# Ten adaLN panels in the inner norm gaps, and decays, samples and turned outputs as 128-row products, in a hybrid decoder step on one core

## What is computed

```python
def _layer(x, c, st, p):
    mod = silu(c) @ p['ada_w'] + p['ada_b']            # 1024 -> 9 * 1024
    sh1, sc1, g1, sh2, sc2, g2, sh3, sc3, g3 = split(mod, 9)
    u = modulate(rmsnorm(x, p['norm_ff1']), sh1, sc1)
    x = x + 0.5 * g1 * ((silu(u @ w1) * (u @ w3)) @ w2)
    u = modulate(rmsnorm(x, p['norm_mix']), sh2, sc2)
    mq, mk, mv, mo, mi, mf, z, xbc, dtp, ga, gb = split(u @ p['w_in'])
    # branch a: causal conv and silu of q and k, mLSTM with matrix memory C (samples start from a state),
    #           head norm, sigmoid(mo), @ w_pa -> ya
    # branch b: causal conv and silu of xbc, state-space scan with decays
    #           lmat = exp(cum[t] - cum[s]), y = (C B^T * lmat) @ (dt x) + exp(cum) * C @ h0, gate, norm, @ w_pb -> yb
    merged = sigmoid(ga) * ya + sigmoid(gb) * yb
    x = x + g2 * (merged @ p['w_out'])
    u = modulate(rmsnorm(x, p['norm_ff2']), sh3, sc3)
    x = x + 0.5 * g3 * ((silu(u @ w1b) * (u @ w3b)) @ w2b)
    return x, states
```

## Time and profile before

| | us |
|---|---|
| median of 3 runs | 1436.12 (1432.69 to 1439.61) |
| the profiled execution | 1435.53 |
| its span, first to last instruction | 1433.8 |

### The profile page before, as it was taken

The page is one execution under the profiler, slowest core; times in us unless marked ns, Lnnn a source line. Parts: engine busy times, 40 slices in busy tenths (PEclk is TensorE's granted clock), DMA queues, the critical chain, the costliest instruction groups (busy, mean ns, idle before and its releaser), DMA issues. The chain is left out here.

```text
span 1433.8 us, 22800 instructions
## 1 busy us (share of the span) xinstructions
PE 1329.5 (93%) x9262; PEld 1199.7 (84%) x9262; DVE 771.7 (54%) x1344; ACT 610.6 (43%) x1070; POOL 146.4 (10%) x282
## 2 busy tenths in 40 slices
PE   5699999997989987888999999999999879999997
PEld 2599999995988855557998878888999879999997
DVE  0544444436975555554368666855365464555542
ACT  3433334224546443434345554544463244333333
POOL 3000000000320011110013121111100010000000
PEclk9799999998999998999999999999999999999999
DMA  9566666764433377893463354463334353544441
GB/s 277 196 206 220 221 218 204 232 228 147 147 95 89 128 269 260 274 319 102 147 206 118 111 162 140 133 196 114 114 102 133 132 176 119 177 147 138 142 144 56
DMA packets 258606, 241.54 MB, mean 168 GB/s; under 512 B 8399, under 2 KB 242215, under 8 KB 258454
## 3 DMA queue, kind: packets, MB, share of 16 engines
q1 hardware_dynamic: 249198, 211.00, 47.2%
q0 software_dynamic: 8832, 28.91, 5.7%
q10 hardware_dynamic: 472, 0.17, 0.0%
HBM read 209.84 MB, written 30.21 MB: 167 GB/s over the span
## 5 line engine op out<-in xcount | busy, mean ns | idle before, releaser
L1817 DVE TENSOR_TENSOR w_lo<-ring,w_hi 128x1024 fp32r<-128x1024 f32 (+1 forms) x264 | 336.1, 1274 | 510.5 <-ACT w_hi L1302 509.4
L1302 ACT ACTIVATE w_hi<-ring 128x1024 fp32r<-128x1024 f32 (+1 forms) x264 | 289.4, 1097 | 604.0 <-PE bank L659 597.2
L659 PE MATMUL bank<-u_hi,w_hi 128*128 128x320 f32 x1536 | 278.6, 325 | 24.7 <-ACT u_hi L1334 19.6
L659 PEld LDWEIGHTS bank<-u_hi,w_hi 128*128 128x128 f32 x1536 | 239.8, 194 | 43.4 <-issue 27.6
L659 PE MATMUL bank<-u_lo,w_hi 128*128 128x320 f32 x1536 | 263.2, 315 | 0.0
L659 PE MATMUL bank<-u_hi,w_lo 128*128 128x320 f32 x1536 | 258.4, 311 | 0.0
L659 PEld LDWEIGHTS bank<-u_lo,w_hi 128*128 128x128 f32 x1536 | 240.2, 193 | 0.0
L659 PEld LDWEIGHTS bank<-u_hi,w_lo 128*128 128x128 f32 x1536 | 235.6, 189 | 0.0
L563 POOL TENSOR_TENSOR arena<-arena 128x320 f32<-128x320 f32 x24 | 20.9, 871 | 653.3 <-ACT arena L1314 640.5
L659 PE MATMUL bank<-arena 32*128 32x128 f32 (+6 forms) x600 | 63.8, 376 | 22.3 <-DMA arena<-in_state_mlstm_C 18.5
L656 PE MATMUL aux<-ident,arena 128*128 128x128 f32 (+5 forms) x389 | 58.6, 274 | 11.3 <-ACT arena L1353 8.9
(11 more groups left out here) (327 smaller groups left out, 1514.9 us busy)
## 6 DMA issues: line engine op xcount, KB each, us to landing
ring<-in_w_in SPq DMA_DIRECT2D x52, 1024.0 KB, 5.2
ring<-in_ff_w SPq DMA_DIRECT2D x44, 1024.0 KB, 5.2
ring<-in_ada_w SPq DMA_DIRECT2D x36, 1024.0 KB, 7.3
ring<-in_ff_w SPq DMA_DIRECT2D x32, 704.0 KB, 4.5
arena<-in_state_mlstm_C SPq DMA_DIRECT2D x32, 512.0 KB, 4.5
out_s_C<-arena POOLq DMA_DIRECT2D x32, 512.0 KB, 4.8
ring<-in_w_pa SPq DMA_DIRECT2D x8, 1024.0 KB, 5.4
arena<-in_state_ssm SPq DMA_DIRECT2D x32, 256.0 KB, 3.7
```

Source lines behind the costliest of these rows:

```text
L659: return nc.tensor.matmul(dst, lhs, rhs, start=first, stop=last)
L1302: nc.scalar.activation(w_hi[v.split_no % 2][:, 0:v.kc, :], panel_part(v), ACT.Copy).then_inc(S["hi_done"], 1)
L1817: V.tensor_tensor(w_lo[r][:, 0:v.kc, :], panel_part(v), w_hi[r][:, 0:v.kc, :].bitcast(FP32), ALU.subtract)\
```

## The change

- Gap 2 has six adaLN panels (26 to 31) instead of three, gap 3 four (32 to 35) instead of two; up1 has 12 instead of 14, down1 six instead of seven, up2 none instead of two.
- `high_ahead` and `low_ahead` take a last unit that they don't go beyond. In down1 and out it is that stage's own last unit. In the gaps ACT makes the next stage's first w_hi between the pairs of tiles, the second one at the end, and DVE the w_lo likewise.
- `norm_high` works by pairs of tiles, `normed` is cut into the reciprocal, a half and a range of u_lo tiles; rows and sums of the panels stand between these parts. The first norm calls the same parts one after the other.
- The decay product takes all 128 rows: rows 0 to 63 of head_pick and cum_rows are filled with zeros by DVE. cum_rows shared its columns with xd_s, which therefore moves over tri and tri_s, no longer used by then.
- The sample products take 128 instead of 96 rows of vp, kpm and st_s, with the last 32 rows filled with zeros by ACT. `turn_head` transposes all 128 rows of the third block.

Of the diff, hunks without their context; the order of the parts inside norm_high and normed is as told above:

```diff
@@ -31,10 +31,9 @@
-ADA_HEAD, ADA_GAP2, ADA_GAP3 = range(0, 8), range(29, 32), range(32, 34)
-ADA_AFTER_UP = dict(zip((3, 5, 9, 11, 15, 17, 21, 23, 27, 29, 33, 35, 39, 41), range(8, 22)))
-ADA_AFTER_DOWN = {2 * a + 1: 22 + a for a in range(7)}
-ADA_AFTER_UP2 = {3: 34, 9: 35}
+ADA_HEAD, ADA_GAP2, ADA_GAP3 = range(0, 8), range(26, 32), range(32, 36)
+ADA_AFTER_UP = dict(zip((3, 7, 11, 15, 17, 21, 23, 27, 31, 35, 39, 41), range(8, 20)))
+ADA_AFTER_DOWN = {2 * a + 1: 20 + a for a in range(6)}
@@ -123,10 +122,7 @@
-    for q in range(2 * KF):
-        order.append(("up2", q))
-        if q in ADA_AFTER_UP2:
-            order.append(("ada", ADA_AFTER_UP2[q]))
+    order += [("up2", q) for q in range(2 * KF)]
@@ -165,6 +161,8 @@
+        with nc.sbuf_tensor("xd_s", [128, 512], FP32) as xd_s:
+            pass
@@ -312,7 +310,6 @@
-        xd_s = part(14592, 512)
@@ -965,7 +962,7 @@
-                    mm(q[32 * g:32 * g + 32, :], st_s[h][0:96, 384 + 32 * g:416 + 32 * g], vp[g][h][0:96, :].bitcast(FP32), True, False)
+                    mm(q[32 * g:32 * g + 32, :], st_s[h][:, 384 + 32 * g:416 + 32 * g], vp[g][h][:, :].bitcast(FP32), True, False)
@@ -985,7 +982,7 @@
-                        ins = mm(pair[:, d, :], kpm[(SB * h + k) % 4][0:96, d * 128:(d + 1) * 128], vp[g][h][0:96, :])
+                        ins = mm(pair[:, d, :], kpm[(SB * h + k) % 4][:, d * 128:(d + 1) * 128], vp[g][h][:, :])
@@ -1013,7 +1010,7 @@
-                turn(x[:, 256:320], nm[0:64, 2, j * 128:(j + 1) * 128], 64).then_inc(S["hn_turned"], 1)
+                turn(x[:, 256:384], nm[:, 2, j * 128:(j + 1) * 128], 128).then_inc(S["hn_turned"], 1)
@@ -1089,7 +1086,7 @@
-                    mm(x[:, 0:448], head_pick[64:128, n:n + 1].to_broadcast([64, 128]), cum_rows[64:128, :], True, False)
+                    mm(x[:, 0:448], head_pick[:, n:n + 1].to_broadcast([128, 128]), cum_rows[:, :], True, False)
@@ -1246,15 +1243,8 @@
-            before = None
-            for u in st.range(("up2", 0), ("up2", 2 * KF - 1)):
-                if u.name == "ada":
-                    ada(u)
-                else:
-                    dense(u, norm=2 if u.q == 0 else None)
-                if before and before.name == "ada":
-                    mod_columns(before)
-                before = u
+            for u in st.of("up2"):
+                dense(u, norm=2 if u.q == 0 else None)
@@ -1291,11 +1281,13 @@
-            def high_ahead(u):
+            def high_ahead(u, last=units[-1]):
+                    if v.n > last.n:
+                        break
@@ -1321,17 +1313,17 @@
-            def norm_high(n, shift):
+            def norm_high(n, shift, pair):
+                tiles = range(2 * pair, 2 * pair + 2)
...
@@ -1401,16 +1394,25 @@
-                high_ahead(u)
+                high_ahead(u, st.at["down1", 2 * KD - 1])
-            for u in st.range(("ada", ADA_GAP2[0]), ("ada", ADA_GAP2[-1])):
-                ada_row(u)
-                if u.q == ADA_GAP2[0]:
-                    root(1)
-            norm_high(1, 3)
+            fill = [st.at["ada", a] for a in ADA_GAP2]
+            ada_row(fill[0])
+            root(1)
+            ada_row(fill[1])
+            ada_row(fill[2])
+            norm_high(1, 3, 0)
+            ada_row(fill[3])
+            norm_high(1, 3, 1)
+            ada_row(fill[4])
+            high_ahead(fill[-1], st.at["qk", 0])
+            norm_high(1, 3, 2)
+            ada_row(fill[5])
+            norm_high(1, 3, 3)
+            high_ahead(fill[-1])
@@ -1498,10 +1500,13 @@
-                copy(st_s[h][64:96, 416:448], st_s[h][32:64, 416:448]).then_inc(S["sx_ready"], 1)
+                ch.inc(copy(st_s[h][64:96, 416:448], st_s[h][32:64, 416:448]))
+                copy(st_s[h][96:128, 384:448], st_s[h][96:128, 0:64], scale=0.0).then_inc(S["sx_ready"], 1)
+                for g in range(2):
+                    ch.inc(copy(vp[g][h][96:128, :], seg_b[96:128, :, :].rearrange("p b t -> p (b t)"), scale=0.0))
@@ -1542,6 +1547,7 @@
+                    ch.inc(copy(kpm[n][96:128, :], seg_b[96:128, 0:4, :].rearrange("p b t -> p (b t)"), scale=0.0))
@@ -1752,19 +1758,23 @@
+                high_ahead(u, st.at["out", KD - 1])
+                square(2, u.own)
+            fill = [st.at["ada", a] for a in ADA_GAP3]
+            ada_row(fill[0])
+            root(2)
+            ada_row(fill[1])
+            norm_high(2, 6, 0)
+            ada_row(fill[2])
+            norm_high(2, 6, 1)
+            ada_row(fill[3])
+            high_ahead(fill[-1], st.at["up2", 0])
+            norm_high(2, 6, 2)
+            norm_high(2, 6, 3)
+            high_ahead(fill[-1])
+            for u in st.of("up2"):
-                square(2, u.own)
-            for u in st.range(("ada", ADA_GAP3[0]), ("ada", ADA_GAP3[-1])):
-                ada_row(u)
-                if u.q == ADA_GAP3[0]:
-                    root(2)
-            norm_high(2, 6)
-            for u in st.range(("up2", 0), ("up2", 2 * KF - 1)):
-                high_ahead(u)
-                if u.name == "ada":
-                    ada_row(u)
-                else:
-                    up(u, KF)
+                up(u, KF)
@@ -1807,11 +1817,13 @@
-            def low_ahead(u):
+            def low_ahead(u, last=units[-1]):
+                    if v.n > last.n:
+                        break
@@ -1830,18 +1842,21 @@
-            def normed(n, shift):
+            def inverse_root(n):
...
+            def normed(n, shift, half):
...
+            def normed_low(n, first, end):
...
@@ -1908,15 +1926,27 @@
-                low_ahead(u)
+                low_ahead(u, st.at["down1", 2 * KD - 1])
-            normed(1, 3)
-            for a in ADA_GAP2:
-                mod_add(st.at["ada", a])
+            fill = [st.at["ada", a] for a in ADA_GAP2]
+            inverse_root(1)
+            mod_add(fill[0])
+            normed(1, 3, 0)
+            mod_add(fill[1])
+            normed(1, 3, 1)
+            mod_add(fill[2])
+            normed_low(1, 0, 2)
+            mod_add(fill[3])
+            normed_low(1, 2, 4)
+            low_ahead(fill[-1], st.at["qk", 0])
+            mod_add(fill[4])
+            normed_low(1, 4, KD)
+            low_ahead(fill[-1])
+            mod_add(fill[5])
@@ -2204,6 +2234,7 @@
+                ch.inc(V.tensor_scalar(head_pick[0:64, :], ones[0:64, 0:32], 0.0, None, ALU.mult))
@@ -2226,6 +2257,7 @@
+                ch.inc(V.tensor_scalar(cum_rows[0:64, :], seg_b[0:64, 0:7, :].rearrange("p b t -> p (b t)"), 0.0, None, ALU.mult))
@@ -2401,19 +2433,24 @@
+                low_ahead(u, st.at["out", KD - 1])
+                residual(u, KD)
+            fill = [st.at["ada", a] for a in ADA_GAP3]
+            inverse_root(2)
+            mod_add(fill[0])
+            normed(2, 6, 0)
+            mod_add(fill[1])
+            normed(2, 6, 1)
+            mod_add(fill[2])
+            normed_low(2, 0, 2)
+            mod_add(fill[3])
+            normed_low(2, 2, 4)
+            low_ahead(fill[-1], st.at["up2", 0])
+            normed_low(2, 4, KD)
+            low_ahead(fill[-1])
+            for u in st.of("up2"):
-                residual(u, KD)
-            normed(2, 6)
-            for a in ADA_GAP3:
-                mod_add(st.at["ada", a])
-            before = None
-            for u in st.range(("up2", 0), ("up2", 2 * KF - 1)):
-                low_ahead(u)
-                if u.name != "ada":
-                    up(u)
-                if before and before.name == "ada":
-                    mod_add(before)
-                before = u
+                up(u)
```

More of the change, by code:

```diff
@@ L1322, in root @@
                 nc.scalar.activation(rs[:, :], aux[0][:, 0:T], ACT.Sqrt, bias=eps_col[:, 0:1], scale=1.0 / D).then_inc(S["root_ready"], 1)
-            def norm_high(n, shift):
-                for half in range(2):
-                    act.wait_ge(S["xr_ready"], 2 * n + half + 1)
-                    for kc in range(4 * half, 4 * half + 4):
-                        nc.scalar.activation(u_t[:, kc, 0:TP], u_t[:, kc, 0:TP], ACT.Identity, bias=mod[:, shift * KD + kc, 0:1],
-                                             scale=gain[:, kc, 0:1]).then_inc(S["u_ready"], 1)
-                    for kc in range(4 * half, 4 * half + 4):
-                        act.wait_ge(S["u_ready"], n * KD + kc + 1)
-                        act.wait_ge(S["us_ready"], 2 * n + half + 1)
-                        nc.scalar.activation(u_hi[:, kc, :], u_t[:, kc, :], ACT.Copy).then_inc(S["u_hi_ready"], 1)
+            def norm_high(n, shift, pair):
+                tiles = range(2 * pair, 2 * pair + 2)
+                act.wait_ge(S["xr_ready"], 2 * n + pair // 2 + 1)
+                for kc in tiles:
+                    nc.scalar.activation(u_t[:, kc, 0:TP], u_t[:, kc, 0:TP], ACT.Identity, bias=mod[:, shift * KD + kc, 0:1],
+                                         scale=gain[:, kc, 0:1]).then_inc(S["u_ready"], 1)
+                act.wait_ge(S["us_ready"], 2 * n + pair // 2 + 1)
+                for kc in tiles:
```

(29 more changed lines are left out.)

## The result

The changed kernel takes 1425.44 us (median of 5 runs, 1425.18 to 1429.22) against 1436.12 us before; the ratio of the two is 0.9919, 95% interval 0.9895 to 0.9943. That is 11.6 us faster, between 8 and 15. A second set of runs of it, beside other runs of the kernel before, gave 1424.24 us and 0.9910 (0.9888 to 0.9931). The time lies inside the range of the prediction (1410 to 1427), 7 us above its 1418: about two thirds of the 17.8 us arrived.

The account below looks back on a forecast made before the run. PE bounds the dense streams and state-space phases, DVE and ACT chains the norm gaps. 7.0 + 1.4 + 0.4 + 9.0 + 0.5 - 0.5 = 17.8 us off 1435.53, median 1418 us, range 1410 to 1427.

Parts of the forecast that it names:

- the 17.8 us: Whole kernel: forecast gain summed over streams, gaps 2 and 3, decays, samples and turned outputs, less the zero rows.

## What to carry to other kernels

Cover for small copies isn't the engine's idle share in a stage but the slack just behind the place where they are put: look at what the next instruction in that engine's row releases, and whether it waited at all. Set-up work such as zero rows belongs where its engine is known to idle, or on an engine that is idle anyway. And when work is moved into a gap, vary the amount: the first pieces can cost less than they save and the last one more, when a buffer ring sets the limit.

## What the runs showed of the hardware

- GpSimd needs 1.8 us for a zero region of 32 partitions by 512 columns where ScalarE needs 0.57, and 0.98 us for 32 by 256 where ScalarE needs 0.41. Made ahead of time it cost nothing measurable all the same:

```profile
427.19 10.68 POOL L599 TENSOR_SCALAR vp<-seg_b 32x512 fp32r<-32x512 f32 x6
...
463.01 3.92 POOL L599 TENSOR_SCALAR kpm<-seg_b 32x256 fp32r<-32x256 f32 x4 [23.86 <-issue]
```

- Going from 64 to 128 rows paid up to 0.77 us a group in the decays, which stand between 128-row products. It paid nothing measurable in the 16 turned outputs, which stand there too, and going from 96 to 128 rows paid nothing among the sample products.
- A stretch of low clock over the same instructions lasted 7, 10 or 14 us, and a second one, which cost 1.5 us, came and went between kernels with the same instructions there. Two profiles that differ by 2 or 3 us in one stage need such a look at the clock before an edit is blamed.
